# Expert outputs put back at their tokens by TensorE, two experts at a time, instead of through DRAM

## The reference

```python
def _hier_moe(h, w_group, b_group, w_router, b_router, w1, w3, w2):
...
    top_p, top_i = lax.top_k(e_prob, TOP_K)                  # two experts for each token
    top_p = top_p / jnp.sum(top_p, axis=-1, keepdims=True) * g_prob[rows, g_sel][:, None]
...
    def expert_block(args):
        xb, e = args
        hid = jax.nn.silu(xb @ w1[e]) * (xb @ w3[e])
        return hid @ w2[e]
...
    out = jax.ops.segment_sum(ys * slot_w[:, None].astype(ys.dtype), slot_tok, num_segments=n_tok + 1)[:n_tok]
...
        x = x + _hier_moe(_rmsnorm(x, norm_ffn[l]), w_group[l], ...)
    return _rmsnorm(x, final_norm)
```

## Time and profile before

| | us |
|---|---|
| median of 3 runs | 1423.31 |
| profiled execution, its time | 1424.24 |
| profiled execution, its span | 1422.6 |
| PE busy in the span | 1223.8 (86%) |
| VectorE busy | 527.9 (37%) |
| ScalarE busy | 387.3 (27%) |
| GpSimd busy | 92.2 (6%) |
| weight pieces of the experts | 198 of 1 MB |

### The profile page before, as it was taken

The page is one execution under the profiler, slowest core; times in us unless marked ns, Lnnn a source line. Parts: engine busy times, 40 slices in busy tenths (PEclk is TensorE's granted clock), DMA queues, the critical chain, the costliest instruction groups (busy, mean ns, idle before and its releaser), DMA issues. The chain is left out here.

```text
span 1422.6 us, 15467 instructions
## 1 busy us (share of the span) xinstructions
PE 1223.8 (86%) x6254; PEld 828.3 (58%) x6254; DVE 527.9 (37%) x948; ACT 387.3 (27%) x638; POOL 92.2 (6%) x118
## 2 busy tenths in 40 slices
PE   6999999999999988999998864997777489887782
PEld 5887997897687766888886532333333133333330
DVE  4333444667857387445365434110100001010004
ACT  6222232235443432243253220121111112111112
POOL 1000000000000000000000003111111101111100
PEclk9999999999999999999999986999999789999996
DMA  7322213112123212323331069999999979999994
GB/s 266 112 88 76 75 60 115 64 60 82 45 71 107 89 67 100 137 90 107 115 113 66 0 270 322 366 409 408 416 417 407 419 310 396 406 416 415 411 401 184
DMA packets 50470, 301.54 MB, mean 212 GB/s; under 512 B 8882, under 2 KB 9282, under 8 KB 20320
## 3 DMA queue, kind: packets, MB, share of 16 engines
q1 hardware_dynamic: 41792, 281.06, 51.1%
q0 software_dynamic: 8080, 17.41, 3.7%
q10 hardware_dynamic: 528, 2.10, 0.4%
HBM read 296.50 MB, written 12.93 MB: 218 GB/s over the span
## 5 line engine op out<-in xcount | busy, mean ns | idle before, releaser
L1769 PE MATMUL e_u<-w_raw,xT 128*64 128x512 f32 x1056 | 244.0, 608 | 62.1 <-DMA w_raw<-in_w 58.7
L1769 PEld LDWEIGHTS e_u<-w_raw,xT 128*64 128x64 f32 x1056 | 81.6, 139 | 219.7 <-issue 215.6
L2048 DVE SCALAR_TENSOR_TENSOR tn<-tn,e_u 64x512 f32<-64x512 f32 x32 | 21.7, 679 | 429.5 <-ACT tn L1979 429.5
L286 DVE TENSOR_TENSOR s_lo<-s_raw,s_hi 128x2048 fp32r<-128x2048 f32 (+1 forms) x68 | 138.5, 2037 | 42.5 <-ACT s_hi L281 41.5
L281 ACT CAST s_hi<-s_raw 128x2048 fp32r<-128x2048 f32 (+1 forms) x68 | 115.8, 1703 | 104.6 <-PE pz L529 34.7
L1779 PE MATMUL e_y<-w_raw,hidT 128*64 128x512 f32 x528 | 121.9, 604 | 15.4 <-ACT hidT L1974 15.0
L513 PE MATMUL pz<-hT_hi,s_hi 128*128 128x512 f32 x256 | 103.7, 405 | 10.1 <-DVE s_lo L286 10.1
L497 PE MATMUL pz<-hT_hi,s_hi 128*128 128x512 f32 x256 | 102.9, 402 | 0.0
L1969 ACT COPY xT<-e_x 128x512 f32<-128x512 f32 x32 | 18.7, 585 | 306.5 <-PE e_x L1754 306.5
L513 PE MATMUL pz<-hT_hi,s_lo 128*128 128x512 f32 x256 | 101.0, 394 | 0.0
L513 PE MATMUL pz<-hT_lo,s_hi 128*128 128x512 f32 x256 | 100.9, 394 | 0.0
(11 more groups left out here) (355 smaller groups left out, 1904.9 us busy)
## 6 DMA issues: line engine op xcount, KB each, us to landing
w_raw<-in_w SPq DMA_DIRECT2D x198, 1024.0 KB, 27.3
s_raw<-in_w_mix SPq DMA_DIRECT2D x30, 1024.0 KB, 4.8
s_raw<-in_w_gb SPq DMA_DIRECT2D x32, 768.0 KB, 4.2
s_raw<-in_w_out_pieces SPq DMA_DIRECT2D x4, 1024.0 KB, 5.0
w_raw<-ys_scratch SPq DMA_DIRECT2D x8, 512.0 KB, 6.6
x_sb<-in_x SPq DMA_DIRECT2D x4, 512.0 KB, 4.7
rel_bias<-in_rel_tiles POOLq DMA_DIRECT2D x8, 256.0 KB, 3.1
decay<-in_decay POOLq DMA_DIRECT2D x8, 256.0 KB, 4.0
```

The lines of the kernel that those rows point to most:

```text
L286: nc.vector.tensor_tensor(w_lo[n % 2][:, 0:w], w_raw[n % 2][:, 0:w], w_hi[n % 2][:, 0:w].bitcast(F32), ALU.subtract).then_inc(w_split, 1)
L1769: m = nc.tensor.matmul(ps_u[o][lo:lo + FIRST, :], xT[b][:, k * FIRST:(k + 1) * FIRST], raw[j][:, kk * FF:(kk + 1) * FF], start=k == 0, sto ...
L2048: nc.vector.scalar_tensor_tensor(tn[:], tn[:], 1.0, ps_u[b][0:FIRST, :], ALU.add, ALU.mult).then_inc(s_hm, 1)
```

## The change

Outputs no longer go through DRAM. For a pair of experts g = (2g, 2g + 1), whose 64 + 64 slots fill 128 rows:

- Routing keeps `pos` and makes `wq`, the weight of every token for every expert (three products more). `idy` goes.
- `weights_of(g)` on VectorE builds `m`, for each token of a tile a row of 128 slots that holds the token's weight at its slot: eight operations of 128x64.
- `turn_weights(g)` on TensorE transposes its four tiles, and `weights_in(g)` on ScalarE copies the result to `st`.
- `y_copy` copies the output of an expert in two halves into `yc`, so that a pair's outputs lie as 128 rows of 1024.
- `unit(g, u)` on TensorE multiplies one tile of `st` by one half of `yc`: one plain fp32 matmul, 128 rows, 128 columns, 512 moving. `add(g, u)` on VectorE adds its 128x512 result to `x_sb`. There are eight units per pair, four in the period of each expert: behind each half of `up(q)`, before `down(q - 1)` and behind it. Two PSUM banks, `ps_c`, take units and turned weights in turn, so a unit waits for the addition two before it (`bank_free`). The units of a pair run three and four experts behind its first expert.
- The job does the same by itself, with its own weights `m_job`, turns, copy and eight units, all inside the job loop. Its list and its rows are fetched while experts 8 to 10 run, and its indices and `m_job` made by `job_ids(0)` on VectorE after expert 9. Inside the loop the next job's list, indices and rows are fetched and made again, `job_ids(r + 1)`, whether or not there is one. The job table is also written 128 times over to DRAM in pieces of 16 bytes (`job_of_all`), so that each partition can load its job's row.
- At the end the last pair's units are added tile by tile, and the final pass follows as before.

The core of the diff:

```diff
@@ -113,9 +113,9 @@
...
-        ys_dram = nc.dram_tensor("ys_scratch", [SLOTS, D], F32).ap()
         list_dram = nc.dram_tensor("list_scratch", [EXPERTS * LIST, 1], I32).ap()
         jobs_dram = nc.dram_tensor("jobs_scratch", [1, P], I32).ap()
+        job_of_all = nc.dram_tensor("jobs_wide", [JOBS + 1, P, 4], I32).ap()
...
@@ -1665,6 +1667,12 @@
     do.after(nc.vector.reciprocal(sm[:, 4, :], sm[:, 4, :]))
     do.after(nc.vector.tensor_scalar(wsel[:, 0, :], sm[:, 4, :], 0.5, None, ALU.mult))
     do.after(nc.vector.tensor_tensor(wsel[:, 1, :], wsel[:, 0, :], sm[:, 3, :], ALU.mult))
+    wide = [P, T, EXPERTS]
+    do.after(nc.vector.tensor_tensor(junk[:, 0, :, :], hot[:, 0, :, :],
+                                     wsel[:, 0, :].unsqueeze(2).to_broadcast(wide), ALU.mult))
+    do.after(nc.vector.tensor_tensor(junk[:, 1, :, :], hot[:, 1, :, :],
+                                     wsel[:, 1, :].unsqueeze(2).to_broadcast(wide), ALU.mult))
+    do.after(nc.vector.tensor_tensor(wq[:], junk[:, 0, :, :], junk[:, 1, :, :], ALU.add))
     dve.wait_ge(s_pc, 1)
     do.after(nc.vector.tensor_copy(pos[:], ps_p[:, 0:T * EXPERTS].rearrange("p (t e) -> p t e", t=T)))
...
 s_tx, s_xT, s_tn, s_h3, s_hm, s_hd, s_ht, s_hT, s_yo = (
     sem("e_" + n) for n in ("tx", "xT", "tanh", "h3", "hm", "hd", "ht", "hT", "yo"))
 s_lst, s_ids, s_jobs, s_jobs_out, s_dve = (sem("e_" + n) for n in ("list", "ids", "jobs", "jobs_out", "dve"))
-o_xs, o_ys, o_tx, o_xT, o_up, o_tn, o_h3, o_id, o_hm, o_hd, o_ht, o_hT, o_dn, o_yo, o_xo = (
-    sem("o_" + n) for n in ("xs", "ys", "tx", "xT", "up", "tanh", "h3", "id", "hm", "hd", "ht", "hT",
+o_xs, o_tx, o_xT, o_up, o_tn, o_h3, o_id, o_hm, o_hd, o_ht, o_hT, o_dn, o_yo, o_xo = (
...
@@ -1743,8 +1757,23 @@
     if q >= 0:
         eng.wait_ge(s_used[slot(q, n)], USE[q])
-def y_of(t, ch):
-    return raw[slot(END, t)][:, ch * D:(ch + 1) * D]
+def unit_bank(g, u):
+    return ps_c[(9 * g + u) % 2]
+def bank_free(eng, g, u):
+    before = 9 * g + u - 2
+    if before >= 0:
+        g0, u0 = divmod(before, 9)
+        if u0:
+            eng.wait_ge(c_a, 8 * g0 + u0)
+        else:
+            eng.wait_ge(c_S, g0 + 1)
+def units_at(q, i):
+    g, u = ((q - 3) // 2, i) if q % 2 else ((q - 4) // 2, 4 + i)
+    return (g, u) if g >= 0 else None
 junk = raw[slot(END, T)][:, 0:D]
 final_gain = raw[slot(END, T)][:, D:2 * D]
...
@@ -1814,15 +1845,8 @@
     ring(MID, MID + DEEP - 1)
     sp.wait_ge(o_xo, n + 1)
     ring(MID + DEEP - 1, EXPERTS)
-    for n_ in range(PIECES):
-        consumed(sp, END, n_)
+    consumed(sp, END, W2A)
     sp.dma_start(final_gain, bass.AP(a["rows"].tensor, 0, [[0, P], [1, D]])).then_inc(f_gain, 16)
-    for b in range(2):
-        sp.wait_ge(s_ys[b], 16 * (EXPERTS // 2))
-    for t in range(T):
-        for ch in range(2):
-            r = ch * N + t * P
...
@@ -1854,42 +1870,45 @@
         for t in range(T):
             pool.indirect_dma_start(list_dram, bass.IndirectOffsetOnAxis(destu[:, ch, t:t + 1], 0),
                                     asg[:, ch, t:t + 1], None).then_inc(s_scattered, 16)
+    def list_of(r):
+        j = pool.value_load(jobs_dram[0:1, bass.ds(r * 4, 1)], min_val=0,
+                            max_val=(EXPERTS * LIST - FIRST) // LIST_UNIT)
+        for lo in (0, FIRST):
+            pool.dma_start(ibl[lo:lo + FIRST, :], list_dram[bass.ds(j * LIST_UNIT, FIRST), :].bitcast(U32)
+                           ).then_inc(s_lst, 16)
+        pool.dma_start(jb[:], job_of_all[bass.ds(r, 1), :, :].rearrange("o p q -> (o p) q")
+                       ).then_inc(s_lst, 16)
+    def rows_of_job():
+        pool.indirect_dma_start(xo[:], None, xn_dram,
+                                bass.IndirectOffsetOnAxis(ibx[0:FIRST, :], 0),
+                                bounds_check=last_x, oob_is_err=False).then_inc(o_xs, 16)
     for q in range(MID):
         fetch(q + 2)
-        if q:
-            store(q - 1)
-    store(MID - 1)
-    pool.wait_ge(s_scattered, 16 * 2 * T)
-    pool.wait_ge(s_jobs_out, 16)
+        if q == LIST_AT:
+            pool.wait_ge(s_scattered, 16 * 2 * T)
+            pool.wait_ge(s_jobs_out, 16)
+            pool.wait_ge(s_jobs_wide, 16)
+            list_of(0)
+        if q == LIST_AT + 2:
+            pool.wait_ge(s_ids, 1)
+            pool.wait_ge(o_zero, 1)
+            rows_of_job()
     n = pool.value_load(jobs_dram[0:1, 2:3], min_val=0, max_val=MAX_EXTRA)
...
@@ -1907,6 +1926,7 @@
             m1, m3 = up_half(half, q % 2, q % 2, slot(q, n1), slot(q, n3))
             m1.then_inc(s_used[slot(q, n1)], 1)
             m3.then_inc(s_used[slot(q, n3)], 1)
+            combine(q, half)
     def turn_hidden(q):
         pe.wait_ge(s_hd, q + 1)
...
@@ -1915,10 +1935,31 @@
     def down(q):
         pe.wait_ge(s_hT, q + 1)
-        wait(pe, s_yo, q - 1)
+        wait(pe, s_yo, 2 * (q - 1))
         for half, n in enumerate((W2A, W2B)):
             landed(pe, q, n)
             down_half(half, q % 2, q % 2, slot(q, n)).then_inc(s_used[slot(q, n)], 1)
+    def turn_weights(g):
+        bank_free(pe, g, 0)
+        pe.wait_ge(c_m, 8 * g + 8)
+        for t in range(T):
+            last = nc.tensor.transpose(unit_bank(g, 0)[:, t * P:(t + 1) * P], m[:, t, :], ident[:])
+        last.then_inc(c_st, 1)
+    def unit(g, u):
+        t, h = divmod(u, 2)
+        bank_free(pe, g, u + 1)
+        if u == 0:
+            pe.wait_ge(c_S, g + 1)
+            pe.wait_ge(s_yo, 4 * g + 4)
+        nc.tensor.matmul(unit_bank(g, u + 1)[:], st[:, t * P:(t + 1) * P], yc[g % 2][:, h, :],
+                         start=True, stop=True).then_inc(c_u, 1)
+    def combine(q, i):
+        at = units_at(q, i)
+        if at is not None:
+            unit(*at)
     def experts(lo, hi):
         turn_rows(lo)
@@ -1928,7 +1969,16 @@
                 turn_rows(q + 1)
             if q > lo:
                 turn_hidden(q - 1)
+            combine(q, 2)
+            if q > lo:
                 down(q - 1)
+            combine(q, 3)
+            if q % 2 == 0 and q >= 2:
+                turn_weights((q - 2) // 2)
+        if hi == EXPERTS:
+            for i in range(4):
+                combine(hi, i)
+            turn_weights((hi - 2) // 2)
         turn_hidden(hi - 1)
         down(hi - 1)
...
-            m.then_inc(o_dn, 1)
-            pe.wait_ge(o_yo, r + 1)
+                y = down_half(half, 0, 0, OVER + n_)
+            y.then_inc(o_dn, 1)
+            pe.wait_ge(o_m, r * 4 + 4)
+            pe.sem_inc(s_turn, 1)
+            for t in range(T):
+                last = nc.tensor.transpose(ps_c[0][0:FIRST, t * P:(t + 1) * P], m_job[:, t, :], ident[:])
+            last.then_inc(o_st, 1)
+            pe.wait_ge(o_S, r + 1)
+            pe.wait_ge(o_yo, r * 2 + 2)
             pe.sem_inc(o_xo, 1)
+            for u in range(2 * T):
+                t, h = divmod(u, 2)
+                if u >= 2:
+                    pe.wait_ge(o_ca, r * 8 + u - 1)
+                nc.tensor.matmul(ps_c[u % 2][:], st_job[:, t * P:(t + 1) * P], y_job[:, h, :],
+                                 start=True, stop=True).then_inc(o_cu, 1)
+            pe.wait_ge(o_ca, r * 8 + 8)
+            pe.sem_inc(s_turn, 1)
         pe.nop()
     experts(MID, EXPERTS)
+    for u in range(2 * T):
...
         consumed(act, q, W2B)
-        wait(act, s_ys[q % 2], 16 * (q // 2))
-        nc.scalar.copy(yo[q % 2][:], ps_y[q % 2][:]).then_inc(s_yo, 1)
+        wait(act, c_u, 8 * (g - 1))
+        for h in range(2):
+            nc.scalar.copy(yc[g % 2][lo:lo + FIRST, h, :], ps_y[q % 2][h * FIRST:(h + 1) * FIRST, :]
+                           ).then_inc(s_yo, 1)
+    def weights_in(g):
+        act.wait_ge(c_st, g + 1)
+        wait(act, c_u, 8 * g)
+        nc.scalar.copy(st[:], unit_bank(g, 0)[:]).then_inc(c_S, 1)
     def experts(lo, hi):
         rows_in(lo)
@@ -1995,6 +2070,10 @@
             halves(q)
             if q > lo:
                 y_copy(q - 1)
+            if q % 2 == 0 and q >= 2:
+                weights_in((q - 2) // 2)
+        if hi == EXPERTS:
+            weights_in((hi - 2) // 2)
         hidden_in(hi - 1)
         y_copy(hi - 1)
...
@@ -2041,9 +2123,34 @@
     do.after(nc.vector.memset(jobs[:, 3:4], 0.0))
     nc.vector.tensor_copy(jobsi[:], jobs[:]).then_inc(s_jobs, 1)
+    def weights_of(g):
+        wait(dve, c_st, g)
+        for t in range(T):
+            for i in range(2):
+                q = 2 * g + i
+                nc.vector.tensor_scalar(m[:, t, i * FIRST:(i + 1) * FIRST], slot_no[:, 0:FIRST],
+                                        pos[:, t, q:q + 1], wq[:, t, q:q + 1], ALU.is_equal, ALU.mult
+                                        ).then_inc(c_m, 1)
+    def add(g, u):
+        t, h = divmod(u, 2)
+        dve.wait_ge(c_u, 8 * g + u + 1)
+        wait(dve, c_a, 8 * (g - 1) + u + 1)
+        xt = x_sb[:, t, h * FF:(h + 1) * FF]
+        return nc.vector.tensor_tensor(xt, unit_bank(g, u + 1)[:], xt, ALU.add).then_inc(c_a, 1)
+    def combine(q, i):
+        at = units_at(q, i)
```

(85 more changed lines are left out.)

80 lines of the change are left out of this document (33 added, 47 removed).

## The result

The changed kernel takes 1490.61 us (median of three runs, 1487.91 to 1491.42), 1.0461 times as long as before (95% interval 1.0439 to 1.0483). Slower was forecast, but 1438, with a range up to 1452: the direction came as worked out, and most of the size did not. The profiled execution's span is 1486.0, where the sum gave 1436.4; 49.6 us are to be found.

The account below looks back on a forecast made before the run. DMA (share 1.01) bounds the kernel; the bound passes to TensorE at 15.85 us per expert. Last `down` 23.1 us later, 9.3 given back by store, reload and additions: span 1436.4, with 1.6, 1438 us; range 1426 to 1452.

Parts of the forecast that it names:

- jobs_wide: Job table's 2176 16-byte pieces on SP's ring ahead of expert 3's weights: costs nothing, at most 2 us.
- the software queue's 5.5 us: Nearest row for the small pieces: 6.1% of 90 us, 870 to 960, with 1024 four-byte pieces; scaled, at most 11.7.
- 9.5 of cover: Second half of `up(6)`: TensorE would arrive at 968.6, its weights at 959.06, so a delay up to 9.5 us is hidden.
- I take 0.07: Each of five added changes per expert between 64-column and full-width matmuls costs 0.07 us, 0.35 per expert.
- the old work of 11.86: TensorE's existing work per expert without the hidT wait: 6.97 + 0.94 + 0.47 + 3.48 us.
- the turns' 0.27: Four weight turns per pair on TensorE, forecast at 0.45 us per pair, 0.22 per expert.
- a whole tail: Upper bound for one change of matmul width: a record's 0.59 us against the pitch of 0.43, 0.16.
- rival C: Each change of matmul width is a full drain of 0.16 us: 13 more, 1451 us; chance 0.22.
- a row that had room for it: Sixteen 64-column matmuls take 6.84 us, full-width turns begin after 6.97: 0.13 for a change, part maybe the last issue.
- I gave the job itself 1.3: Job's old 20.1 us held 3.0 (`up`) and 1.3 (`down`) of low clock; only the 3.0 was given back.
- the wait for the job's list: Behind the job, VectorE in `job_ids(r + 1)` waits for lists POOL asks for late: 2.5 us charged, bounds 0 and 6.
- Rival A: Whole kernel: DMA keeps the bound and the end comes faster, 1403 us, if a unit costs under 0.75; chance 0.07.

Follow-up runs that it names:

- e1: Changed kernel with the job table no longer written 128 times over; job rows read from the plain table in 128 pieces on POOL's queue: 1476.01 us.
- e2: Changed kernel with an expert's four units in twos, two behind the whole of `up` and two before `down`: 1475.54 us.
- e3: Changed kernel with each unit issued as two matmuls of 64 columns into the halves of its bank: 1461.76 us.
- e5: Changed kernel without the 2176 small pieces and with each unit as two matmuls of 64 columns: 1448.73 us, ratio 1.0177 to the kernel before.
- e6: Changed kernel without the 2176 small pieces, pairs' units on operands rounded to fp32r, job's units still fp32: 1411.56 us, ratio 0.9902 to the kernel before.
- e8: Changed kernel without the fetch of a next job inside the loop (list, rows, indices): 1486.03 us, ratio 1.0425 to the kernel before.

## Why the prediction was wrong in size

**The step that failed first: jobs_wide, "so nothing, at most 2 us".** It cost 15.4 us in span (12.6 of waiting, 2.8 of low clock), 14.6 by e1. I bounded it from the software queue's 5.5 us for everything it carried, 11.7 scaled, under 9.5 of cover. But those four-byte pieces were written by another queue, and the row tells what that queue's packets took, not what such a DMA does to the ring behind it. The ring stood for about 24 us (until about 923), twice the upper bound of 11.7; one of the 2176 pieces went by every 11 ns. Bytes and packet time don't explain it: from 900 to 918 the DMA engines were busy for a share of 0.29 only. What limits such pieces to this pace stays open.

**The second: "I take 0.07" for each of five changes.** I had left out those between units and 64-row transposes. Each of the four units has one change in front and one behind, and of these eight the old work of 11.86 held one; and they cost 0.15 and 0.20, in front of the unit behind `turn_hidden` 0.11. In place of 0.35 the period has 1.15 (16.70 less 11.86, 3.42 and the turns' 0.27). With the turns' 0.05 that is 24.7 us more over 29 experts. The upper bound of 0.16, "a whole tail", was nearly right for going in and too low for coming out, so that rival C at 1451 was also too low. The rule that changes cost time is borne out: e2 halves the changes by order alone, e3 leaves only those beside transposes, at twice the instructions, and 15.1 and 28.9 us go. The Trainium skill, "TensorEngine Tiling (Array Packing)", section Key Properties, says that a change of tiling mode drains TensorE. The traces agree as far as the cost goes, 0.11 to 0.20 us at each; no run here shows that it is a drain. I had named the rule and sided with a row that had room for it.

**The third: low clock after the job.** I gave the job itself 1.3 and expected `up(16)` at full speed; its first half took 3.0 more, and two units behind the wait for VectorE 1.8 more.

The rest of the sum held, the job in part by luck: its units took 7.67 us at the full clock in the changed kernel's profile, and 11.5 to 13.4 us, at 0.5 to 0.6 of it, in those of e1, e2, e3, e5, e6 and e8, which issue the same eight. The profiled run was the fastest of the three, 2.7 under the median. The first 2.1 us are mostly the first gather, which landed later (TensorE's first transposes at 881.14 for 879.67); why wasn't tested. In span, against the forecast:

| stretch | forecast | measured | difference |
|---|---|---|---|
| to the point where `up(3)` could begin | 916.9 | 919.0 | 2.1 |
| wait for expert 3's weights, and low clock | 0 | 15.4 | 15.4 |
| `up(3)` to the last `down` before the job | 209.7 | 220.8 | 11.1 |
| job, to `up(16)` | 31.6 | 32.1 | 0.5 |
| `up(16)` to the last `down` | 259.8 | 280.2 | 20.4 |
| tail | 18.4 | 18.5 | 0.1 |

The last but one holds 13.6 of changes, 3.0 of low clock, 0.4 of the wait for the job's list (2.5 forecast, 2.9 measured) and 1.8 of low clock behind it. What is left, 1.6, is for the most part a wait of 1.3 us (at 1460.23) for VectorE, which builds the last pair's weights first. Right were: that the bound passes from DMA to TensorE; that a unit is 0.855 and four of them don't fit beside the weights' pace; that the early rows are worth little; and the tail, which did what the change is for: first addition 2.5 us after the last `down`, final pass 16.0. That gives back 9.2 us of what costs 72.6.

Rival A (1403) needed a unit under 0.75 us. e6, without the small pieces, made it so, at 0.43 with the changes, and came to 1411.56: its mechanism was right, its price missing.

Not tried: the wide table in fewer or larger pieces, or on another queue, which would show whether their number or their place in front of the weights counts for more; and how the low clock in the job can be avoided without changing the work. It varied between profiles of like kernels (7.67 to 13.38 us for the same eight units), so single differences of 4 to 6 us between these versions are not read as causes.

## What to carry to other kernels

Before filling idle time of an engine, write out the pace of both sides: here TensorE had 3.2 to 3.6 us per expert, and 3.4 us of scatter matmuls, with everything around them, took them all; then each further tenth counts in full, 29 times. Keep one width of matmul in a run, or issue the odd ones in the width of their neighbours. And count the pieces of a DMA, not only its bytes, above all when it stands in front of the big loads on the same queue: here the broadcast cost nothing that was seen as 128 pieces of a small load on POOL's queue (e1), and 15 us as 2176 pieces in front of the weights.

## What the runs showed of the hardware that was not expected

- 34 KB in 2176 pieces held a queue for about 24 us: 16 GB/s at a DMA share of 0.29, where 392 GB/s pass without them.
- A change from 64-column to 128-column matmuls cost 0.15 us and the change back, or from a unit to 64-row transposes, 0.20, also when nothing else is waited for; two 64-column halves with the same moving operand ran in the time of one full-width matmul, 0.855.
- The DMA share is no proof of a bound: from 1220 to 1420 it reads 0.99 in the changed kernel, where TensorE never waits and only 381 GB/s move; before, 1.01 went with 412 to 416.
- After an idle time of 12.5 us `up(3)` took 2.8 us more at the low clock. In the job, whose idle times were 0.5 to 2.2 us, the granted clock fell as well, in some profiles sooner than in others: the same eight units ran at 1.00, 0.61 and 0.52 of it, in 7.67, 11.71 and 13.38 us.
